# Undivided rows for the first products of a block's input and feed-forward stages

## The reference

```python
def rms_norm(x, g):
    xf = x.astype(jnp.float32)
    y = xf * lax.rsqrt(jnp.mean(xf * xf, axis=-1, keepdims=True) + RMS_EPS)
    return (y * g.astype(jnp.float32)).astype(x.dtype)

def sgu_mixer(h, w_in, b_in, g_v, w_s, b_s, w_out):
    z = jax.nn.gelu(h @ w_in + b_in, approximate=False)
    u, v = jnp.split(z, 2, axis=-1)
    v = rms_norm(v, g_v)
    v = v.reshape(B, n_blk, SGU_CHUNK, SGU_GROUPS, SGU_GROUP_DIM)
    v = jnp.einsum('gts,bnsgc->bntgc', w_causal, v) + b_s.T[None, None, :, :, None]
    y = u * v.reshape(B, S, SGU_HALF)
    return y @ w_out

def conv_ffn(h, w_up, conv_w, conv_b, w_down):
    z = h @ w_up
    z = sum(zp[:, j:j + S] * conv_w[j] for j in range(CONV_WIDTH)) + conv_b
    gate, val = jnp.split(z, 2, axis=-1)
    return (jax.nn.silu(gate) * val) @ w_down

    h = x
    for i in range(DEPTH):
        hn = rms_norm(h, norm_mix_g[i])
        ...
            h = h + sgu_mixer(hn, sgu_w_in[j], sgu_b_in[j], sgu_g_v[j],
                              sgu_w_s[j], sgu_b_s[j], sgu_w_out[j])
        ...
        h = h + conv_ffn(rms_norm(h, norm_ffn_g[i]), ffn_w_up[i], ffn_conv_w[i],
                         ffn_conv_b[i], ffn_w_down[i])
```

## Time and profile before

| | us |
|---|---|
| median of 3 runs | 2678.5 |
| lowest and highest | 2677.86, 2684.62 |
| the profiled execution, its time | 2680.04 |
| its span | 2678.2 |
| TensorE busy | 2289.2 (85%) |
| VectorE busy | 1163.7 (43%) |
| ScalarE busy | 855.7 (32%) |

### The profile page before, as it was taken

One profiled execution on the slowest core, in us unless ns is written; L12 is line 12 of the kernel. 1 busy time (PEld: TensorE's weight loads), 2 busy tenths in 40 slices (PEclk: granted clock), 3 DMA queues, 4 the chain that ended last, 5 costly groups with the idle time before them and its releaser, 6 DMA issues. The chain is left out here.

```text
span 2678.2 us, 32481 instructions
## 1 busy us (share of the span) xinstructions
PE 2289.2 (85%) x13804; PEld 1677.3 (63%) x13804; DVE 1163.7 (43%) x1844; ACT 855.7 (32%) x1275; POOL 163.3 (6%) x174
## 2 busy tenths in 40 slices
PE   6898999976997886589999989977987688888784
PEld 5776888855765875368888867756976433333331
DVE  4336665347474565556664343755333411111112
ACT  4324443237653222344442244634122110000010
POOL 0000000000001120000000000002310011111110
PEclk9888999988999777689999999965758799989898
DMA  5112222222210101112222323121014499999996
GB/s 192 66 52 74 95 97 94 92 88 87 79 63 13 18 14 33 71 63 95 99 101 87 107 86 111 47 65 23 2 48 178 198 418 419 412 405 409 401 405 229
DMA packets 106741, 377.26 MB, mean 141 GB/s; under 512 B 54976, under 2 KB 55760, under 8 KB 67680
## 3 DMA queue, kind: packets, MB, share of 16 engines
q1 hardware_dynamic: 84992, 296.44, 29.9%
q10 hardware_dynamic: 9216, 67.11, 6.0%
q0 software_dynamic: 12384, 11.58, 1.5%
HBM read 375.31 MB, written 27.53 MB: 150 GB/s over the span
## 5 line engine op out<-in xcount | busy, mean ns | idle before, releaser
L589 PE MATMUL ps<-xh,wh 128*128 128x512 f32 x1384 | 554.1, 400 | 84.2 <-DVE wl L555 32.6
L590 PE MATMUL ps<-xl,wh 128*128 128x512 f32 x1384 | 548.6, 396 | 0.0
L591 PE MATMUL ps<-xh,wl 128*128 128x512 f32 x1384 | 547.5, 396 | 0.0
L555 DVE TENSOR_TENSOR wl<-raw,wh 128x2048 fp32r<-128x2048 f32 (+2 forms) x127 | 264.3, 2081 | 294.6 <-ACT wh L549 294.6
L589 PEld LDWEIGHTS ps<-xh,wh 128*128 128x128 f32 x1384 | 266.0, 192 | 160.6 <-issue 57.6
L3272 PE MATMUL ps<-egu,XT 128*64 128x512 f32 x1088 | 273.4, 660 | 81.8 <-DMA egu<-e_up 78.1
L591 PEld LDWEIGHTS ps<-xh,wl 128*128 128x128 f32 x1384 | 265.4, 192 | 57.2
L590 PEld LDWEIGHTS ps<-xl,wh 128*128 128x128 f32 x1384 | 266.0, 192 | 55.7 <-issue 0.7
L549 ACT ACTIVATE wh<-raw 128x2048 fp32r<-128x2048 f32 (+2 forms) x127 | 220.2, 1735 | 83.1 <-PE ps L960 69.5
L3272 PEld LDWEIGHTS ps<-egu,XT 128*64 128x64 f32 x1088 | 94.9, 152 | 236.8 <-issue 225.2
L3290 DVE TENSOR_TENSOR HIDT<-ps,SIL 128x256 f32<-128x256 f32 x34 | 14.4, 424 | 348.6 <-ACT SIL L3282 348.6
(11 more groups left out here) (495 smaller groups left out, 3232.8 us busy)
## 6 DMA issues: line engine op xcount, KB each, us to landing
egu<-e_gate SPq DMA_DIRECT2D x68, 1024.0 KB, 15.0
egu<-e_up SPq DMA_DIRECT2D x68, 1024.0 KB, 25.3
ed<-e_down ACTq DMA_DIRECT2D x64, 1024.0 KB, 9.6
raw<-up SPq DMA_DIRECT2D x44, 1024.0 KB, 4.9
raw<-down SPq DMA_DIRECT2D x32, 704.0 KB, 4.1
raw<-rwkv_kr SPq DMA_DIRECT2D x8, 1024.0 KB, 4.8
raw<-in_dn SPq DMA_DIRECT2D x8, 1024.0 KB, 4.9
raw<-sgu_u SPq DMA_DIRECT2D x4, 1024.0 KB, 8.4
```

The lines of the kernel that those rows point to most:

```text
L555: e.tensor_tensor(K.WL[s][:, 0:n], K.RAW[r][:, 0:n], K.WH[s][:, 0:n].bitcast(F32), SUB).then_inc(*K.w_low.mark(i))
L589: e.matmul(o, h[:, q, k], x_high[:, k], start=k == 0, stop=False)
L590: e.matmul(o, h[:, q, k], x_low[:, k], start=False, stop=False)
L591: last = e.matmul(o, l[:, q, k], x_high[:, k], start=False, stop=k == KT - 1)
```

## The change

The feed order is values first: `sgu_v` stands ahead of `sgu_u` in the list of weight items and of bank uses. The first transfers are the parameters, the first weight item, x, the second weight item, and then the rest.

Input: `open_high_act` and `open_low_dve` split H times gain, without the root. The first value chunk (`first_values_pe`) is multiplied from it with k as the outer loop, then the norm's sums are made (`first_norms_pe`): one as a row for tokens along the free side, and four columns `RC` for tokens on the partitions. The root is applied to the products: values get it in the instruction that adds the bias (`scalar_tensor_tensor` with `RC`), gates in a new multiplication with the root's row `T[5]` ahead of Gelu. All the mixer's products read undivided rows. The gates are made in two halves with the first four mixing tiles between, and the other four behind.

Feed-forwards: `sgu_o` and `rwkv_o` end with `open_residual_act` and `open_residual_dve`, which split H times gain into new buffers `XHA`, `XLA` as each tile is ready. The first OPEN = 4 up tiles read these; the norm's product with ones stands in the midst of the first item, at k = 4. The other 40 tiles read rows divided as before. The four are multiplied by the root in PSUM ahead of the convolution.

```diff
 def sgu_sp(K, e):
     A = K.A
+    e.dma_start(K.PRM[:, :], A["params"]).then_inc(*K.param_in.landing("params"))
+    load_weights(K, e, 0, 1)
     for i in range(4):
         e.dma_start(K.H[:, 2 * i:2 * i + 2], A["x"][256 * i:256 * i + 256].rearrange("(k p) t -> p k t", p=128)).then_inc(
-    e.dma_start(K.PRM[:, :], A["params"]).then_inc(*K.const_in.landing("params"))
+    load_weights(K, e, 1, 2)
     e.dma_start(K.CST[:, :], A["consts"]).then_inc(*K.const_in.landing("consts"))
-    load_weights(K, e, 0, 2)
...
+def open_high_act(K, e, stage, k, gain, token, high):
+    e.wait_ge(*token)
+    e.activation(high[:, k], K.H[:, k], ACT.Identity, bias=K.prm("zero"), scale=gain).then_inc(*K.x_high.mark(stage, k))
+def open_low_dve(K, e, stage, k, gain, high, low):
+    e.wait_ge(*K.x_high(stage, k))
+    e.scalar_tensor_tensor(low[:, k], K.H[:, k], gain, high[:, k].bitcast(F32), MUL, SUB).then_inc(*K.x_low.mark(stage, k))
...
 def sgu_pe(K, e):
-    e.wait_ge(*K.const_in("consts"))
-    norm_pe(K, e, "n_mix0")
-    gemm_pe(K, e, "sgu_u", "sgu_u", KT, K.XH, K.XL)
-    gemm_tok_pe(K, e, "sgu_v", "sgu_v", range(4), 256, "sgu_u")
+    first_values_pe(K, e)
+    first_norms_pe(K, e)
+    gemm_tok_pe(K, e, "sgu_v", "sgu_v", range(1, 4), 256, "sgu_v")
+    gemm_pe(K, e, "sgu_u", "sgu_u", 4, K.XH, K.XL, ready="sgu_v")
     e.wait_ge(*K.sgu_in("bs"))
     e.wait_ge(*K.pool_sgu("ws"))
+    mixed_pe(K, e, 0)
+    gemm_pe(K, e, "sgu_u", "sgu_u", 4, K.XH, K.XL, ready="sgu_v", begin=4)
+    mixed_pe(K, e, 4)
     gemm_pe(K, e, "sgu_o", "sgu_o", KT, K.XH, K.XL)
...
+def open_residual_dve(K, e, stage, l, m):
+    u = K.u[stage] + m
+    e.wait_ge(*K.gemm_sum(stage, m))
+    e.tensor_tensor(K.H[:, m], K.ps[:, u % 8], K.H[:, m], ADD).then_inc(*K.dve_out.mark(stage, m))
+    K.board.empty(u, K.dve_out(stage, m))
+    open_low_dve(K, e, f"open{l}", m, K.prm("ffng", 8 * l + m), K.XHA, K.XLA)
+    sumsq_dve(K, e, f"n_ffn{l}", m)
...
 def ffn_pe(K, e, l):
-    norm_pe(K, e, f"n_ffn{l}")
-    gemm_pe(K, e, up, up, 2 * FT, K.XH, K.XL)
+    gemm_pe(K, e, up, up, 2, K.XHA, K.XLA, ready=f"open{l}", between=lambda K, e: norm_pe(K, e, f"n_ffn{l}"))
+    gemm_pe(K, e, up, up, OPEN - 2, K.XHA, K.XLA, ready=f"open{l}", begin=2)
+    gemm_pe(K, e, up, up, 2 * FT - OPEN, K.XH, K.XL, begin=OPEN)
...
 def ffn_dve(K, e, l, norm):
+    for m in range(OPEN):
+        u = up_use(K, l, m)
+        e.wait_ge(*K.gemm_sum(up, m))
+        e.tensor_tensor(K.ps[:, u % 8], K.ps[:, u % 8], K.T[5], MUL).then_inc(*K.conv.mark(up, m, "divided"))
```

More of the change, by code:

```diff
@@ L580, in gemm_pe @@
         for k in range(KT):
-            if i == 0:
+            if i == begin // mt:
                 e.wait_ge(*K.x_low(ready or stage, k))
+                if k == 4 and between:
+                    between(K, e)
             for q in range(mt):
@@ L821, in sgu_pool, with first_values_pe, first_norms_pe, mixed_pe @@
                     pattern=[[0, 16], [1, 128]], channel_multiplier=-1).then_inc(*K.pool_sgu.mark("ws"))
[L824 to L832 removed]
+def first_values_pe(K, e):
+    _, n, _, _, s = K.items[0]
+    h, l = (x[s][:, 0:n].rearrange("p (k j) -> p k j", k=KT) for x in (K.WH, K.WL))
+    e.wait_ge(*K.w_low(0))
+    for k in range(KT):
+        e.wait_ge(*K.x_low("sgu_v", k))
+        for n in range(4):
+            o = K.ps[:, (K.u["sgu_v0"] + n) % 8, 0:256]
+            xh, xl = K.XH[:, k, 128 * n:128 * n + 128], K.XL[:, k, 128 * n:128 * n + 128]
+            e.matmul(o, xh, h[:, k], start=k == 0, stop=False)
+            e.matmul(o, xl, h[:, k], start=False, stop=False)
+            last = e.matmul(o, xh, l[:, k], start=False, stop=k == KT - 1)
+            if k == KT - 1:
+                last.then_inc(*K.gemm_sum.mark("sgu_v", 0, n))
+    K.gemm_sum.also("item", 0)
+def first_norms_pe(K, e):
+    e.wait_ge(*K.const_in("consts"))
+    e.wait_ge(*K.sumsq("n_mix0", KT - 1))
+    u = K.u["n_col"]
+    for n in range(4):
+        last = e.matmul(K.ps[:, u % 8, n:n + 1], K.T[0][:, 128 * n:128 * n + 128], K.cst("ones", 1), start=True, stop=True)
+    last.then_inc(*K.norm_sum.mark("n_col"))
+    u = K.u["n_mix0"]
+    e.matmul(K.ps[:, u % 8], K.cst("ones", 128), K.T[0], start=True, stop=True).then_inc(*K.norm_sum.mark("n_mix0"))
+def mixed_pe(K, e, begin):
+    for m in range(begin, begin + 4):
+        u = K.u["sgu_mix4" if begin else "sgu_mix"] + m - begin
         b = u % 8
@@ L878, in sgu_act @@
     for m in range(KT):
-        x_high_act(K, e, "sgu_o", m, K.T[m % 4], K.dve_mix("y", m), K.XH, [K.gemm_sum("sgu_v", 3, 3)])
+        if m % 2 == 0 and m:
+            next_high(K, e, K.first["sgu_u"] + m // 2)
+        e.wait_ge(*K.dve_mix("u", m))
+        e.activation(K.U[:, m], K.T[3 + m % 2], ACT.Gelu, bias=K.prm("bu", m)).then_inc(*K.act_out.mark("sgu_u", m))
+    for m in range(KT):
+        x_high_act(K, e, "sgu_o", m, K.T[m % 3], K.dve_mix("y", m), K.XH, [K.gemm_sum("sgu_u", 7)])
     for m in range(KT):
@@ L882, in sgu_act @@
             next_high(K, e, K.first["sgu_o"] + m // 2)
-        residual_act(K, e, "sgu_o", "n_ffn0", m)
+        open_residual_act(K, e, "sgu_o", 0, m)
     K.board.point("ACT", "sgu")
 def sgu_dve(K, e):
+    weight_low(K, e, 0)
+    e.wait_ge(*K.param_in("params"))
+    for k in range(KT):
+        open_low_dve(K, e, "sgu_v", k, K.prm("mixg", k), K.XH, K.XL)
+    weight_low(K, e, 1)
     for k in range(KT):
         sumsq_dve(K, e, "n_mix0", k)
[L890 to L895, removed]
+    e.wait_ge(*K.rows_in("rows"))
+    e.wait_ge(*K.rstd("n_col", "r"))
     for ch in range(4):
-        next_low(K, e, K.first["sgu_v"] + ch)
+        if ch:
+            next_low(K, e, K.first["sgu_v"] + ch)
+        if ch == 3:
+            next_low(K, e, K.first["sgu_u"])
         for n in range(4):
@@ L927, in sgu_dve, with up_use @@
             next_low(K, e, K.first["sgu_o"] + m // 2)
-        residual_dve(K, e, "sgu_o", "n_ffn0", m)
+        open_residual_dve(K, e, "sgu_o", 0, m)
     K.board.point("DVE", "sgu")
+OPEN = 4
+AHEAD = {0: 2, 1: 3, 3: 4, **{i: i for i in range(5, FT)}}
+def up_use(K, l, m):
+    return K.u[f"up{l}"] + m if m < 2 else K.u[f"up{l}2"] + m - 2 if m < OPEN else K.u[f"up{l}{OPEN}"] + m - OPEN
 def ffn_sp(K, e, l):
```

126 lines of the change are left out of this document (81 added, 45 removed), and 2 rows, old and new, of the table held.

## The result

| | before | after |
|---|---|---|
| median, us | 2678.34 (4 runs) | 2643.83 (4 runs) |
| lowest and highest | 2677.86, 2684.62 | 2638.45, 2647.25 |
| the profiled execution, its span | 2678.2 | 2642.6 |

The ratio is 0.987, with an interval of 0.9845 to 0.9895. The change makes the kernel faster by 34.5 us, and the forecast was 58.9. The direction was right, the size was not: 2643.8 lies outside the range of 2612 to 2635.

The account below looks back on a forecast made before the run. TensorE, busy 85% of the span, was taken as the bound, losing time to waits and low clock. Mixer -34.7 and two borders -24.2 sum to -58.9: 2678.5 to 2619.6 us, range 2612 to 2627, up to 2635 with most rivals.

Parts of the forecast that it names:

- Mixing: 26.5 gained ... if the clock stays high: Last value product to first `sgu_o` product: 42.1 us shrink to 15.6 of mixing at the full clock, 26.5 gained.
- rival A: Mixing runs at the low clock all the same, costing 11 to 18 us in all; 2631 to 2638, chance 0.14.
- 2.8 to 5.6 us on VectorE ahead of the next weight split, which has 5 to spare: Feed-forward borders: four divisions in PSUM, 0.7 us each or twice that, fit ahead of the next weight split.
- Rival D: Feed-forwards: divided rows or third item's weights come late, each border gives 6 us instead of 12; 2632, chance 0.05.
- The start: Kernel's beginning: weights land at 6.9, first product at 11.8 instead of 22.81; 11.0 us gained.
- Rival B: First transfers share the rate instead of coming in turn, so the start is 5.2 us later; 2625, chance 0.05.
- The norm's sums on the path: After the first value chunk: the norm's sums now take TensorE's time, 2.1 us lost.
- the second chunk's successor: First values: next weights' split waits behind root, Gelu and squares, 12.3 us against a chunk's 11.5; 0.8 lost (0 to 3).
- The bank wait of 1.4 at the fifth mixing tile: Mixing: the fifth tile waits for the first's bank, emptied on VectorE behind gate divisions six and seven; 1.4 us lost.
- The sum of squares at the border: Feed-forward border: ready at 5.1 us, just covered by 24 products of 5.4; 1.5 later would cost 1.1.
- The gain at a border without the late split: Each of two borders to the feed-forwards: undivided tiles follow at once, 12.1 us gained, 24.2 for both.
- Rival C: Slower than before: the low clock from mixing stays until the end of `sgu_o`; 2700, chance 0.02.

Follow-up runs that it names:

- e1_rows128: Changed kernel with both factors of the mixing's bias product on 128 rows instead of 16, rows 16 to 127 zero: 2635.80 us, ratio 0.9826.
- e5_same: The changed kernel itself, unedited, timed and traced again: 2643.26 us, ratio 0.9857.
- e6_twice16: Changed kernel with each bias product of the mixing made twice, on 16 rows: 2660.52 us, ratio 0.9923.
- e2_ahead: Changed kernel with the weight splits one pair earlier from the fifth pair of up tiles on: 2626.90 us, ratio 0.9803.
- e4_mixer_only: Changed kernel's mixer with the norm, its product and the feed-forwards of the kernel before: 2649.71 us, ratio 0.9877.
- e8_x_first: Changed kernel with the first transfers in the old order (x, parameters, then weights): 2646.86 us, ratio 0.988.
- e3_all: Changed kernel with bias factors on 128 rows, splits one pair earlier, and three gate multiplications ahead of the last two gate divisions: 2620.13 us, ratio 0.9773.
- e7_twice128: Changed kernel with each bias product made twice, factors on 128 rows, rows 16 to 127 zero: 2641.56 us, ratio 0.9853.

## Why the prediction was wrong in size, and where it was right

**The step "Mixing: 26.5 gained ... if the clock stays high" failed.** The forecast wrote the condition down, put it into rival A with a chance of 0.14, and took the other side because pairs of 128- and 32-row products had stayed at 1.00. The condition didn't hold. Against the same stretches of e1_rows128 the low clock cost after 0.9 in the first group (9.11 less 8.20), 0.8 in the gates behind it (22.86 less 22.05), 6.1 in the second group (14.47 less 8.36) and 1.8 in `sgu_o` (45.45 less 43.62): 9.7, nearly all of the 9.9 that the mixer lacks, and 1.3 below the lower end of rival A's 11 to 18. That two groups of 8 us between dense work are too short to fall was the argument; the first one fell in after, e5_same and e6_twice16, and not in e2_ahead, e4_mixer_only and e8_x_first. The row that spoke for A was in the forecast: mixing had stayed at 0.50 for 27 us of being busy. It was outweighed by the earlier trace rows, 32 rows and a product of 0.64 us, which are neither the rows nor the share of time of this case. A stretch of one's own kernel that shows the clock low while busy is nearer than one elsewhere that shows it high.

The Trainium skill ("TensorE: Matmul & The Clock Gate", Why this matters for your kernels) asks for TensorE to be kept busy, and by that rule the clock would have come back. The runs disagree: e6_twice16 is busy for all of 21.02 us at a mean of 0.53.

**The step "2.8 to 5.6 us on VectorE ahead of the next weight split, which has 5 to spare" failed.** The divisions themselves were at the cheap end, 2.49 for four. But the 5 us, for which the forecast shows no rows, were meant for the next split, and the one that came late is three items on. The forecast has no term for a pair. It costs 9.9 us of a chain between two engines, 6.6 without a split, against TensorE's 10.9: enough to keep up, and not enough to make good a start that the root, the divided rows and the divisions put 27.5 us behind the border (177.56 to 205.07), before the seventh item's split was due. Rival D had this as "the third item's weights come late", 0.05 and 6 us a border; it was the seventh item, and 6.7 and 7.1 us a border. What the forecast names as wrong, "if TensorE waits for weight splits among the first six items", missed even the place by one.

With the second failure alone the kernel takes 2635.80 (e1_rows128), just above the range; with the first alone 2626.90 (e2_ahead), inside it, though there the clock fell less in the profiled execution than in after. The forecast treated A and D as alternatives; they are independent, and both at once, 2643 to 2650 by its own prices, stood nowhere.

**Right, by the forecast's own steps:**

- The start: first product at 11.62, forecast 11.8; the landing of the weights 6.57, forecast 6.9; transfers in turn, shown by e8_x_first. Rival B falls. (Behind the first piece of x stood 5.0 MB by the sizes given, not 4.5; nothing is worked out from it.)
- The norm's sums on the path: TensorE stood 0.40 for them and worked on them from 25.92 to 27.35, when the next chunk began: 1.8, forecast 2.1. From 11.62 to 62.40 are 50.78 us; the forecast's pieces make 51.3, and the 0.8 of it for the second chunk's successor didn't come.
- A mixing tile at the full clock takes 2.06 (8.24 for four), not 1.95, which makes 0.9 us for eight. Half of a low-clock tile was too low: the tile takes 3.91 at the low clock, so not all in it halves.
- The bank wait of 1.4 at the fifth mixing tile: 1.38 measured, and gone when VectorE's order is changed.
- The sum of squares at the border: VectorE finished it at 182.85, 5.3 behind the last product of `sgu_o`, where 5.1 was forecast, and TensorE came to it at 183.00. Covered by 0.15 us.
- The gain at a border without the late split: 12.3 and 12.2 in e3_all, forecast 12.1.
- The rest of the kernel: it took over the gain, 718.0 and 1252.7 against 716.9 and 1253.9.
- Rival C, slower: the low clock went with the dense products for 3.9 us of `sgu_o`, not for all of it.

With both failed conditions made true, and the 1.4 of the bank wait taken away, e3_all comes to 2620.13; the forecast, with that wait, was 2619.6. By its ratio to before, 0.9773, it would be 2617.5 beside a before of 2678.34. In the spans, e3_all gained 60.4 where the sum without the wait makes 60.3. So the terms of the sum were right within a us or two, and the two conditions under it were not.

## What to carry to other kernels

When work of a thin kind (few rows of the array) is moved between dense products, ask the trace of before which clock that very work has had while busy, and, if it was low, pad its rows with zeros; here that cost nothing that the runs show and gave 8 to 11 us, and 19 where the thin work was doubled. Where two engines hand each tile to and fro in order, take the price of an item from one start to the next in the timeline, not from busy times, and when the first one starts late, follow the queue until it has caught up: the wait comes where the slack runs out, here at the seventh item. Two conditions of a forecast that don't depend on each other need a case in which both fail.

## What the runs showed of the hardware

In this mixing the granted clock depends on the rows that TensorE's bias products use. In six groups of mixing with the bias products on 128 rows (e1_rows128, e3_all, e7_twice128) the clock stayed at 1.00. In the twelve groups of the six profiled executions with 16 rows (after, e2_ahead, e4_mixer_only, e5_same, e6_twice16, e8_x_first) it fell in nine, at different places: in the second group every time, in the first in after, e5_same and e6_twice16. The products are as long at a given clock with either number of rows: two instructions of a bias product take 1.02 to 1.12 us at 1.00. Why the first group falls in some traces and not in others isn't shown: the traces of after, e2_ahead and e4_mixer_only are alike up to there within half a us, and no run here tells what decides it. In all six executions with 16 rows the second group stands behind a wait of 1.38 us; with 128 rows the same wait brought no fall (e1_rows128, e7_twice128), but no run has 16 rows without it, so whether it helps the fall there isn't shown. Nor is it shown whether 64 or 32 rows would do.
